# Strassen's scheme, one level, for the gate and up projections of three feed-forward layers in a one-core Trainium2 kernel

## What is computed

```python
def rms_norm(x, g):                       # as the reference computes it, float32
    return x * rsqrt(mean(x * x, -1) + 1e-6) * g

x = x + merged @ w_out
h2 = rms_norm(x, norm2_g)
ffn = (silu(h2 @ w_ffn_gate) * (h2 @ w_ffn_up)) @ w_ffn_down
x = x + ffn
```

## Time and profile before

| what | value |
|---|---|
| median of 3 runs (lowest to highest) | 3846.43 us (3845.4 to 3850.24) |
| span of the profiled execution | 3844.5 us |
| busy in it: PE, weight loads, DVE, ACT, POOL | 95%, 75%, 52%, 43%, 10% |
| mean granted TensorE clock | 0.968 |
| first feed-forward stage (gate/up), 1134.6 to 1376.3 | 241.7 us |

### The profile page before, as it was taken

How to read it: one execution, slowest core, us unless ns; L and a number is a source line. 1 busy time by engine, 2 the same in 40 slices (tenths; PEclk the granted TensorE clock), 3 DMA queues, 4 the chain that set the end, 5 groups by cost and what they waited for, 6 DMA issues and landing times. The chain is left out here.

```text
span 3844.5 us, 52297 instructions
## 1 busy us (share of the span) xinstructions
PE 3642.5 (95%) x20532; PEld 2868.1 (75%) x20532; DVE 1980.4 (52%) x3166; ACT 1634.2 (43%) x2544; POOL 402.0 (10%) x353
## 2 busy tenths in 40 slices
PE   8898889969999999899999999999899999999998
PEld 6456777758878887677777788887687777788887
DVE  5879565584443334655545443333655545443332
ACT  5454432545333334456444433223456445433222
POOL 0027233000001111320000001100020000001100
PEclk9899889979999999999999999999999999999999
DMA  3012001203232232112212232333212212232232
GB/s 124 11 47 61 1 2 62 72 3 123 91 104 94 97 96 91 55 55 72 68 65 87 90 102 93 98 93 95 66 50 73 68 50 99 85 105 93 98 93 77
DMA packets 84161, 289.34 MB, mean 75 GB/s; under 512 B 9200, under 2 KB 9456, under 8 KB 82672
## 3 DMA queue, kind: packets, MB, share of 16 engines
q1 hardware_dynamic: 83520, 283.68, 23.1%
q10 hardware_dynamic: 432, 2.78, 0.2%
HBM read 284.32 MB, written 2.10 MB: 75 GB/s over the span
## 5 line engine op out<-in xcount | busy, mean ns | idle before, releaser
L492 DVE TENSOR_TENSOR weights_lo_r<-raw_weights,weights_hi_r 128x1024 fp32r<-128x1024 f32 (+2 forms) x554 | 637.9, 1152 | 1278.1 <-ACT weights_hi_r L486 1277.8
L486 ACT ACTIVATE weights_hi_r<-raw_weights 128x1024 fp32r<-128x1024 f32 (+2 forms) x554 | 546.7, 987 | 1263.6 <-PE ps L565 1212.5
L564 PE MATMUL ps<-xn_r,weights_hi_r 128*128 128x512 f32 x2688 | 1057.8, 394 | 0.0
L563 PE MATMUL ps<-xn_hi,weights_hi_r 128*128 128x512 f32 x1632 | 670.5, 411 | 46.1 <-DVE xn_r L558 18.3
L565 PE MATMUL ps<-xn_hi,weights_lo_r 128*128 128x512 f32 x1632 | 646.0, 396 | 0.0
L564 PEld LDWEIGHTS ps<-xn_r,weights_hi_r 128*128 128x128 f32 x2688 | 511.6, 190 | 106.1 <-issue 5.3
L563 PE MATMUL ps<-y_r,weights_hi_r 128*128 128x512 f32 x1200 | 469.6, 391 | 2.4 <-PEq L890 2.4
L565 PE MATMUL ps<-y_r,weights_lo_r 128*128 128x512 f32 x1200 | 466.9, 389 | 0.0
L563 PEld LDWEIGHTS ps<-xn_hi,weights_hi_r 128*128 128x128 f32 x1632 | 312.6, 192 | 141.7 <-issue 49.7
L565 PEld LDWEIGHTS ps<-xn_hi,weights_lo_r 128*128 128x128 f32 x1632 | 313.1, 192 | 69.0
L563 PEld LDWEIGHTS ps<-y_r,weights_hi_r 128*128 128x128 f32 x1200 | 225.2, 188 | 53.7 <-issue 6.4
(11 more groups left out here) (575 smaller groups left out, 5328.8 us busy)
## 6 DMA issues: line engine op xcount, KB each, us to landing
raw_weights<-in_w_ffn_dram SPq DMA_DIRECT2D x132, 512.0 KB, 3.7
raw_weights<-in_w_down_dram SPq DMA_DIRECT2D x48, 512.0 KB, 3.5
raw_weights<-in_w_out_dram SPq DMA_DIRECT2D x24, 512.0 KB, 3.5
raw_weights<-in_w_down_dram SPq DMA_DIRECT2D x24, 384.0 KB, 3.1
raw_weights<-in_w_hgrn_dram SPq DMA_DIRECT2D x16, 512.0 KB, 3.5
raw_weights<-in_w_mix_ssm_dram SPq DMA_DIRECT2D x16, 512.0 KB, 3.8
raw_weights<-in_w_a_qk_dram SPq DMA_DIRECT2D x16, 512.0 KB, 3.5
raw_weights<-in_w_mix_a_dram SPq DMA_DIRECT2D x16, 512.0 KB, 3.5
```

The costliest lines, as they stand in the source:

```text
L486: act.activation(self.k.w_hi[:, g % 2, 0:chunk.width], self.k.raw[:, slot, 0:chunk.width], ACT.Copy)\
L492: dve.tensor_tensor(self.k.w_lo[:, g % 2, 0:chunk.width], self.k.raw[:, slot, 0:chunk.width], self.k.w_hi[:, g % 2, 0:chunk.width].bitcast ...
L563: pe.matmul(out, w_hi, x_hi, start=start, stop=False)
L564: pe.matmul(out, w_hi, x_lo, start=False, stop=False)
```

## The change

A gate tile and an up tile are two row blocks of one matrix; contraction steps 1 to 4 and 5 to 8 are two column blocks; tokens 1 to 256 and 257 to 512 are two column blocks of the activations. That is a 2x2 by 2x2 block product. The eight block products (each 4 contraction steps, three passes, 256 tokens) become seven, by the scheme of Strassen in Winograd's form:

- **PE**: per tile seven products `b11 t4 t3 b21 t2 b22 t1` of 12 matmuls of 256 columns, 84 in all, in place of 48 of 512.
- **POOL**: four sums of weight blocks per tile (`weight_sum`, 128x512 each) and both multiplications by `rstd` (L4801 and L4804 of the changed kernel), where there was one.
- **ACT**: `hi` of the first raw chunk (128x1024) and of five operands of 128x512 (`ring_part`), three copies of 256 columns out of PSUM (`take`), SiLU, `hi` of the result.
- **DVE**: `lo` of the same six weight operands, four additions or subtractions of 256 columns of PSUM and a held block (`quarter`), the product of gate and up (now both in SBUF), `lo` of the result.
- **Activations**: `SplitSeven` takes the place of `SplitAhead`. The differences of the token and contraction blocks are made by DVE: `low` blocks (one op of 256 columns per tile), and for tiles 5 to 8 three chained ops of 256 (`triple`); then `hi` and `lo` of `low` and `mid` (512 columns) and of `tri` (768). `SevenTile` does the same for tile 8 in the next stage.
- The stage is written out for 22 tiles (before: a loop); the raw ring is filled by SP after POOL, ACT and DVE have read a pair of chunks.

```diff
+class SplitSeven(Nothing):
...
+    def triple(self, dve, j, done, n):
+
+        t, b = self.seven.tri.full[:, j, :], self.seven.mid.full[:, j, :]
+        dve.scalar_tensor_tensor(out=t[:, 0:HALF], in0=self.x[:, j, HALF:T], scalar=self.k.col(self.weight, j),
+                                 in1=b[:, HALF:T], op0=ALU.mult, op1=ALU.subtract).then_inc(done, 1)
+        dve.wait_ge(done, n + 1)
...
+        dve.tensor_tensor(t[:, T:T + HALF], b[:, 0:HALF], t[:, HALF:T], ALU.subtract).then_inc(done, 1)
...
-def scaled_products(k, name, src, split, gate, rstd, opening):
...
+def strassen_products(k, name, seven, split, gate, rstd, held, ring, opening):
...
+            def last_product(i):
+                pe.wait_ge(ring_ready, 5 * i + 5)
+                pe.wait_ge(quarter_ready, 4 * i + 2)
+                return times(out(i, 3), *part(5 * i + 4), "t4")
...
+            for i in range(1, N):
+                n = 5 * i
+                pe.wait_ge(whole_ready, i)
+                if i >= 2:
+                    pe.wait_ge(taken, 3 * (i - 1))
+                times(out(i, 0), *whole(0), "b11", start=True).then_inc(whole_used, 1)
+                last_product(i - 1).then_inc(ring_used, 1)
+                pe.wait_ge(ring_ready, n + 1)
...
+                times(out(i, 3), *part(n), "t3", start=True).then_inc(ring_used, 1)
+                times(out(i, 1), *whole(1), "b21", start=True).then_inc(whole_used, 1)
+                pe.wait_ge(ring_ready, n + 2)
+                pe.wait_ge(taken, 3 * i + 1)
+                times(out(i, 0), *part(n + 1), "t2").then_inc(ring_used, 1)
+                pe.wait_ge(ring_ready, n + 3)
+                times(out(i, 2), *part(n + 2), "b22", start=True).then_inc(ring_used, 1)
+                pe.wait_ge(ring_ready, n + 4)
+                pe.wait_ge(taken, 3 * i + 2)
+                times(out(i, 0), *part(n + 3), "t1").then_inc(ring_used, 1)
+            last_product(N - 1).then_inc(stream.chunk_used, end - g0)
...
+            for i in range(1, N):
+                second_halves(i - 1)
+                ring_part(5 * i)
+                ring_part(5 * i + 1)
+                ring_part(5 * i + 2)
+                up_first(i - 1)
+                ring_part(5 * i + 3)
+                ring_part(5 * i + 4)
+                dve.wait_ge(gate_scaled, i)
+                dve.wait_ge(quarter_ready, 4 * i)
+                dve.tensor_tensor(dst[:, i - 1, :], gate[:, (i - 1) % 2, :], dst[:, i - 1, :], ALU.mult)\
+                    .then_inc(tile_ready, 1)
+                gate_first(i)
+                next_whole(i + 1)
+                dve.wait_ge(hi_ready, i)
+                split.make_lo(dve, i - 1).then_inc(lo_ready, 1)
...
+            def weight_sum(n, a, b):
+                if n >= RING:
+                    pool.wait_ge(ring_used, n - 3)
+                pool.tensor_tensor(slot(n)[0], a, b, ALU.add).then_inc(sums_made, 1)
...
+            for i in range(1, N):
+                g = gate[:, (i - 1) % 2, :]
+                third(i)
+                pool.wait_ge(quarter_ready, 4 * i - 1)
+                pool.tensor_tensor(g, g, rstd, ALU.mult).then_inc(scaled, 1)
+                fourth(i)
+                pool.wait_ge(gate_ready, i)
+                pool.tensor_tensor(g, g, rstd, ALU.mult).then_inc(gate_scaled, 1)
+                if i + 1 < N:
+                    first_two(i + 1)
```

More of the change, by code:

```diff
@@ L4391, in _, with times @@
-            walk(pe, job, multiply)
+            def times(out, w_hi, w_lo, name, js=range(KH), start=False):
+                for j in js:
+                    x_hi, x_lo = seven.block(name, j)
+                    at = slice(j * P, (j + 1) * P)
+                    for n, (a, b) in enumerate(((w_hi, x_hi), (w_hi, x_lo), (w_lo, x_hi))):
+                        mm = pe.matmul(out, a[:, at], b, start=start and j == 0 and n == 0,
+                                       stop=j == KH - 1 and n == 2, skip_group_check=True)
+                return mm
@@ new lines, in _ @@
+            pe.wait_ge(stream.parts_ready, g0 + 1)
+            times(out(0, 0), *whole(0), "b11", start=True).then_inc(whole_used, 1)
+            most, rest = range(KH - 1), range(KH - 1, KH)
+            times(out(0, 1), *whole(1), "b21", most, True)
+            pe.wait_ge(ring_ready, 1)
+            times(out(0, 3), *part(0), "t3", most, True)
+            pe.wait_ge(taken, 1)
+            pe.wait_ge(ring_ready, 2)
+            times(out(0, 0), *part(1), "t2", most)
+            pe.wait_ge(ring_ready, 3)
@@ new lines, in _ @@
+            times(out(0, 2), *part(2), "b22", most, True)
+            opening.ready(pe)
+            times(out(0, 1), *whole(1), "b21", rest).then_inc(whole_used, 1)
+            times(out(0, 3), *part(0), "t3", rest).then_inc(ring_used, 1)
+            times(out(0, 0), *part(1), "t2", rest).then_inc(ring_used, 1)
+            times(out(0, 2), *part(2), "b22", rest).then_inc(ring_used, 1)
+            opening.sums(pe)
+            pe.wait_ge(taken, 2)
+            pe.wait_ge(ring_ready, 4)
+            times(out(0, 0), *part(3), "t1").then_inc(ring_used, 1)
@@ new lines, in next_whole @@
+            def next_whole(i):
+                arrived(act, i, 0)
+                act.wait_ge(whole_used, 2 * i)
+                made = act.activation(k.w_hi[:, first, :], k.raw[:, (g0 + 2 * i) % AHEAD_RAW, :], ACT.Copy)
+                if i < N:
+                    made.then_inc(whole_hi, 1)
+                else:
+                    made.then_inc(stream.hi_made, end - g0)
+            opening.weigh(act)
+            take_base(0)
+            ring_part(0)
+            opening.split_hi(act)
@@ L4454, in scaled_products, with feed_forward @@
         stream.leave(end)
-        return ScaledEnd(split, gate[:, 1, :], rstd, end)
-def feed_forward(k, spare, early, w_ffn, w_down, opening, weight=None, final=None, product=None):
+        return QuartersEnd(split, gate[:, (N - 1) % 2, :], rstd, held_2, 4 * ((N - 1) % 2) + 3, end)
+def feed_forward(k, spare, early, seven, w_ffn, w_down, opening, weight=None, final=None, product=None):
     with ExitStack() as ctx:
@@ L4495, in stream_plan, with layer_branches @@
     return plan
-def layer_branches(k, n, y, y_lo, early, product, opening):
+def layer_branches(k, n, y, y_lo, early, seven, product, opening):
     at = k.col_at[f"norm1_{n}"][0]
```

372 lines of the change are left out of this document (283 added, 89 removed).

## The result

The changed kernel takes **3992.28 us** (median of four runs, 3987.99 to 3998.81), the kernel before 3845.91 in the same comparison: ratio 1.038, 95% interval 1.0365 to 1.0395. The forecast was 3962 in a range of 3875 to 4015: sign and mechanism held, and the loss is 30 us larger than said. The profiled run spans 3996.7 us against 3844.5.

What follows compares the result with a forecast made beforehand. PE bounds the old gate/up stage; DVE and POOL, excluding each other, would bound the changed one. Three times (31.3 stage + 5.3 block end + 2.0 clock) gives +116 us on 3844.5; with 1.9 median offset, 3962 us, range 3875 to 4015.

Steps and rivals of the forecast that it cites:

- PE's side: Gate/up matmuls of 256 columns start 0.1185 us apart, so PE's 84 per tile take 9.95 us.
- Who collides: In gate/up tiles, POOL's instructions and DVE's with two SBUF inputs exclude each other; the four PSUM-reading quarters are free.
- The sum per tile: Steady gate/up tile: 11.5 us of DVE and POOL exclusive time plus 0.7 of waiting, 12.2 us.
- seven of 0.55, one of 1.10: DVE's exclusive time per gate/up tile: 0.55 us for each 512-column instruction, 1.10 for the 1024-column one.
- Who waits: PE waits 2.2 us per gate/up tile, mostly before `b11`, for the `lo` of `next_whole`.
- The opening: Gate/up stage's first tile up to `b11` of the second: 8.5 products, 1.8 norm sums, 5.5 pauses, 15.8 us.
- the clock: Low-clock windows (1.2 GHz) after the pause and in the first tile add 2 us per stage, bounds 0 and 5.
- The block end: End of w_out: twelve DVE instructions behind the last addition delay the next block by 5.3 us, all PE pause.
- (a): Rival: in gate/up tiles exclusion costs nothing and PE binds at 9.95 us a tile; 3805 us, chance 0.12.
- (b): Rival: shorter holds in gate/up, exclusive time about 10.9 us a tile, near break-even at 3865 us; chance 0.06.
- (c): Rival: DVE and POOL exclude each other for whole instructions, 13.7 us per gate/up tile, 4059 us; chance 0.04.
- (d): Rival: each of the 84 gate/up matmuls costs 0.21 us, 17.6 us per tile, +450 us; chance 0.01.

Runs made afterwards that it cites:

- e2: Changed kernel with POOL's four weight sums and two scalings a gate/up tile replaced by memsets of the same destination, waits and signals kept: 3831.75 us.
- e4: Kernel before the change, with five unused 128x512 sums more on POOL in each gate/up tile: 3848.21 us, ratio 1.0005.
- e3: Changed kernel with POOL's six operations a tile given to DVE from the second tile on, DVE's and ACT's order rearranged: 3861.64 us, ratio 1.0034.
- e5: Changed kernel with DVE's activation-block preparation beside w_out one output tile earlier, and ACT weighing a tile before squaring it: 3990.58 us, ratio 1.0378.
- e9: Changed kernel with only the two scalings a tile given back to DVE, the four weight sums staying on POOL: 3921.69 us, ratio 1.0183.
- e10: Changed kernel with only the four weight sums a tile moved to DVE, the two scalings staying on POOL: 3895.01 us, ratio 1.0114.
- e7: Changed kernel with all POOL's gate/up work on DVE, activation preparation moved earlier, pause and opening rebuilt in PE's order of need: 3834.92 us, ratio 0.9977.

## Why the prediction was right, and where it was off

- **PE's side.** 0.1185 us a matmul and 9.95 us a tile were said; 0.120 and 10.08 came. No slow start per product. This held.
- **Who collides.** POOL's readers with DVE's two-SBUF instructions, not with the quarters: shown by the means (1.42 against 0.68; 0.41 unchanged), by e2 and by e4. The Trainium skill (SBUF — State Buffer, section Who interferes with whom) says the same, and that a GpSimd instruction that only writes SBUF does not contend; e2 agrees (0.686 us beside memsets). The Trainium skill's block for the whole instruction would give 13.7 us a tile, an estimate from the durations in the earlier trace rows; 12.60 were measured.
- **The sum per tile: the mis-sized term.** 11.5 of exclusive time + 0.7 for the wait of POOL's scaling = 12.2; 12.60 came, +0.4, x 63 = 25 us of the missing 30. The step that failed is "seven of 0.55, one of 1.10": what a DVE instruction costs in a full row is the distance of starts, 0.60 and 1.13 (e3), not what it holds. 7 x 0.05 + 0.03 = 0.4. The rest fits: DVE's own list is 7 x 0.60 + 1.13 + 4 x 0.33 = 6.7 us; the stretch, by the means after, is 4 x (1.422 - 0.678) + (1.965 - 1.226) + 2 x (1.77 - 0.68) = 5.9, together 12.6. POOL's holds are 6 x 1.09 = 6.5, of which 0.6 fell beside the quarters at 1246.06 and 1250.06. And the two quarters for which POOL's scaling waits are the 0.7 us that I had put there.
- **Who waits.** PE, once a tile, for `next_whole`, 12.9 us in 8 times, 1.6 each, where 2.2 were said; the rest of the 2.5 us is in small pieces (0.6 ahead of `t4`).
- **The opening.** 15.8 us said; 18.8, 17.5 and 17.6 in the three stages, and 13.4 instead of 12.2 for the tile behind. The three instructions of `triple` came at 1.05, 1.39 and 1.38 (1.4 said) and `ring_part` at 1.75. With nothing of POOL reading (e2) it is 14.1. For the clock 2 us had been set aside; from 1151.68 to 1157.83 it is granted at 0.50, which is 1.2 GHz, after PE had waited 2.98 us, and 28 matmuls take 6.15 us, 0.213 instead of 0.120 each, 2.6 us more in this stage. Opening, clock and the tile behind were said at 15.8 + 2 + 12.2 = 30.0 us and came at 32.2, 30.9 and 31.0; without the 0.4 of that tile's own sum some 1 us a stage is over.
- **The block end.** +5.3 said, 7.02 - 0.87 = +6.15 measured. Named rightly: e5 takes five of the twelve instructions out and the pause falls by 2.8.
- **The sum.** Stage about +43 us (31.3 + 2 said), block end +6.15 (5.3 said), three times that is 147 of the 152 us between the two profiled spans; the last `w_out` matmul came 3.8 us later ahead of the first stage, which the change doesn't explain, since it varies by as much between runs of this study.
- **The rivals.** (a), the cover holds at 3805, needed POOL not to read: e2 is that case, at 3832, with the real openings. (b) at 3865 would have needed short holds; a POOL instruction costs DVE 0.99 us in the changed kernel and 0.88 in e9, which with DVE's own 6.7 comes to about 12 us a tile and not to 10.9. (c) and (d) are refuted by 12.60 and 0.120.

What is not settled: why POOL's hold ends before its recorded end (1.09 of 1.29 us), and how much of the difference between the versions with POOL's sums (the changed kernel, e9) and those without (e3, e10) is due to the other order of ACT's and DVE's lists in e3 and e10.

## What to carry to other kernels

Two engines that shut each other out have one budget, as VectorE and GpSimd have here: before work goes to the idle-looking partner, add both lists (here 6.7 us on DVE and 6 x 1.0 on POOL) and compare with the engine that is to stay the bound. If the sum is over it, the "offloaded" instruction can be cheaper on the busy engine: 0.60 us on DVE against 1.0 us of DVE's time when POOL did it. Count a full engine by distance of starts, not by duration or hold, and once the steady part is right look at the first tile and the pause in front of it, which together were worth 5 to 8 us a stage here.

## What the runs showed of the hardware

- POOL's memsets of 128x512 (0.53 us) leave DVE's two-input instructions at 0.686 us; POOL's sums and products of the same size stretch those that start behind one to 1.77.
- A POOL sum or product of 128x512 keeps such a DVE instruction out for about 1.09 us, the same in the changed kernel, e9 and e10; a DVE instruction with an input in PSUM runs in that time at its 0.41 us.
- POOL is held up as well: a sum is 1.29 us alone and 1.61 to 1.88 on average beside a full DVE, 2.28 for the first scaling in e10.
- In e3 and e7 DVE and PE run at 100.00 and 100.00 in the same 100 us, and neither slows the other: 10.29 us a tile by DVE's list, 0.120 us a matmul.
